# The mLSTM stage of a decoder layer: the next head's K and Q slabs inside a head, the recurrence in pieces between matmuls, states on ScalarE's DMA queue

## What is computed

```python
def _mlstm(q, k, v, i_pre, f_pre, C0, n0, m0):      # per head: q, k 128 wide, v 256 wide
    q = q * (DK ** -0.5)
    def step(carry, inp):                           # one chunk
        C, n, m = carry
        qx, kx, vx, ix, lfx = inp
        b = jnp.cumsum(lfx, axis=-1)
        dlog = jnp.where(causal, b[..., :, None] - b[..., None, :] + ix[..., None, :], -jnp.inf)
        inter = b + m[..., None]
        m_row = jnp.maximum(inter, jnp.max(dlog, axis=-1))
        dw = jnp.exp(dlog - m_row[..., None]); w_inter = jnp.exp(inter - m_row)
        s = jnp.einsum('bhld,bhjd->bhlj', qx, kx) * dw
        num = w_inter[..., None] * jnp.einsum('bhld,bhde->bhle', qx, C) + jnp.einsum('bhlj,bhje->bhle', s, vx)
        nq = w_inter * jnp.einsum('bhld,bhd->bhl', qx, n) + jnp.sum(s, axis=-1)
        h = num / jnp.maximum(jnp.abs(nq), jnp.exp(-m_row))[..., None]
        dec = jnp.exp(b[..., -1] + m - m_row[..., -1])
        wk = jnp.exp(ix + b[..., -1:] - b - m_row[..., -1:])
        C_new = dec[..., None, None] * C + jnp.einsum('bhl,bhld,bhle->bhde', wk, kx, vx)   # n likewise
        return (C_new, n_new, m_new), h
...
ha = _head_rms(ha).reshape(B, T, W_A_V) * g_norm_a * jax.nn.sigmoid(o_a)   # q, k, v, o_a: slices of rmsnorm(x) @ w_in
```

## Time and profile before

| | |
|---|---|
| time, median of 3 runs | 2891.81 us (2891.54 to 2893.38) |
| the profiled execution's own time | 2893.21 us |
| its span | 2891.5 us |
| PE busy | 2632.0 us (91%) |
| PEld busy | 2541.4 us (88%) |
| DVE, ACT, POOL busy | 1156.5, 639.4, 622.6 us (40%, 22%, 22%) |
| `mlstm`, first dense matmul to last output transpose | 978.81 to 1444.43 us of the span |
| mean granted TensorE clock | 0.957 of full |

### The profile page before, as it was taken

How to read it: one execution, slowest core, us unless ns; L and a number is a source line. 1 busy time by engine, 2 the same in 40 slices (tenths; PEclk the granted TensorE clock), 3 DMA queues, 4 the chain that set the end, 5 groups by cost and what they waited for, 6 DMA issues and landing times.

```text
span 2891.5 us, 40600 instructions
## 1 busy us (share of the span) xinstructions
PE 2632.0 (91%) x16191; PEld 2541.4 (88%) x16191; DVE 1156.5 (40%) x1932; ACT 639.4 (22%) x1319; POOL 622.6 (22%) x322
## 2 busy tenths in 40 slices
PE   4379999999999689899779999999999999999997
PEld 2269999999998689788679999999999999999997
DVE  2455655565554132523531141554323223134434
ACT  3235545554554111111100000001001000011112
POOL 2232121212120111111031131342212212112421
PEclk7679999999999899999889999999999999999998
DMA  3021221222110314223141121211111111111211
GB/s 122 17 78 55 63 61 32 71 66 61 32 53 24 84 30 92 49 72 85 20 121 46 44 99 44 105 44 44 44 44 44 49 40 49 47 38 45 74 30 70
DMA packets 235748, 165.23 MB, mean 57 GB/s; under 512 B 23643, under 2 KB 222875, under 8 KB 235583
## 3 DMA queue, kind: packets, MB, share of 16 engines
q1 hardware_dynamic: 235638, 163.64, 20.2%
HBM read 135.84 MB, written 27.76 MB: 57 GB/s over the span
## 4 chain that ended last, share of the span: by engine, by line
PE 45%; DVE 2%; issue 1%; POOL 1%; DMA 1%; ACT 0%; POOLq 0%; DVEq 0%; ACTq 0%
PE bank L227 40%; PE bank L239 4%; PE bank L2247 1%; DVE t_rlo L2383 0%; DMA t_w_raw<-in_w_in_dram 0%; PE bank L2284 0%; POOL t_w_lo L216 0%; DVE t_rhi L2380 0%; DVE hlo L2409 0%; DVE hhi L2406 0%; POOL t_rlo L2095 0%; DMA t_rraw<-HB 0%; PE bank L2159 0%; DVE hraw L2553 0%; DVE t_x L2475 0%
## 5 line engine op out<-in xcount | busy, mean ns | idle before, releaser
L216 POOL TENSOR_TENSOR t_w_lo<-t_w_raw,t_w_hi 128x1024 fp32r<-128x1024 f32 x112 | 270.1, 2412 | 942.6 <-DVE t_w_hi L211 942.6
L227 PE MATMUL bank<-t_rhi,t_w_lo 128*128 128x384 f32 (+1 forms) x1248 | 408.4, 327 | 2.8 <-issue 2.8
L227 PE MATMUL bank<-t_rhi,t_w_hi 128*128 128x384 f32 (+1 forms) x1248 | 408.0, 327 | 0.0
L227 PE MATMUL bank<-t_rlo,t_w_hi 128*128 128x384 f32 (+1 forms) x1248 | 407.9, 327 | 0.0
L227 PE MATMUL bank<-hhi,t_w_lo 128*128 128x384 f32 (+1 forms) x1224 | 400.1, 327 | 2.6 <-POOL t_w_lo L216 2.6
L227 PE MATMUL bank<-hhi,t_w_hi 128*128 128x384 f32 (+1 forms) x1224 | 400.3, 327 | 0.0
L227 PE MATMUL bank<-hlo,t_w_hi 128*128 128x384 f32 (+1 forms) x1224 | 400.1, 327 | 0.0
L227 PE MATMUL bank<-hhi,b_w_lo 128*128 128x384 f32 (+1 forms) x768 | 270.7, 352 | 10.1 <-POOL b_w_lo L216 10.1
L227 PE MATMUL bank<-hlo,b_w_hi 128*128 128x384 f32 (+1 forms) x768 | 252.6, 329 | 0.0
L227 PE MATMUL bank<-hhi,b_w_hi 128*128 128x384 f32 (+1 forms) x768 | 252.3, 329 | 0.0
L227 PEld LDWEIGHTS bank<-t_rhi,t_w_lo 128*128 128x128 f32 x1248 | 235.1, 188 | 3.5 <-issue 3.3
(11 more groups left out here) (371 smaller groups left out, 4333.0 us busy)
## 6 DMA issues: line engine op xcount, KB each, us to landing
b_w_raw<-in_w_in_dram SPq DMA_DIRECT2D x32, 512.0 KB, 4.0
t_w_raw<-in_w_up_dram SPq DMA_DIRECT2D x32, 512.0 KB, 3.8
t_w_raw<-in_w_down_dram SPq DMA_DIRECT2D x32, 512.0 KB, 3.8
a_w_raw<-in_w_in_dram SPq DMA_DIRECT2D x24, 512.0 KB, 3.9
t_w_raw<-in_w_in_dram SPq DMA_DIRECT2D x16, 512.0 KB, 3.6
b_gam<-ROWS_B SPq DMA_DIRECT2D x8, 576.0 KB, 4.9
b_eg<-ROWS_B SPq DMA_DIRECT2D x8, 576.0 KB, 3.8
b_kb<-ROWS_B SPq DMA_DIRECT2D x8, 576.0 KB, 3.6
```

The lines of the kernel that those rows point to most:

```text
L216: pool.tensor_tensor(self.lo[j % 2][:, 0:kt, :], self.raw[j % self.rs][:, 0:kt, :], self.hi[j % 2][:, 0:kt, :], ALU.subtract).then_inc(sel ...
L227: ins = pe.matmul(out, a[:, k, :], b[:, k, :], start=(start and k == 0 and i == 0), stop=(stop and k == kt - 1 and i == 2))
```

## The change

All of it is in `mlstm`. The slabs get names (`K_`, `Q_`, `VA_`, `VB_`, `OA_`, `OB_`), and:

- The turn of head h now makes VA, VB, OA, OB of head h and K, Q of head h+1. K and Q of head 0 stand ahead of the turns with a bank order of their own (`FB`), and the last head has one too (`LB`). TensorE waits for ScalarE's copies of Q ahead of the first and of the last turn.
- `scan_all` becomes a generator, `scan_steps`. `woven` makes a product group in pieces of 9, 9 and 6 matmuls and runs one step after each: 8 chunks and the sample chunk in OB's nine pieces, the 8 sample products in K's. In the last head the sample products stand bare.
- `matrices` for three chunks follows each group of OA; `outputs` of head h-1 follows each group of VA(h). The gated outputs are written into the gate's buffers instead of V0 and V1. VectorE's and GpSimd's work is ordered accordingly.
- ScalarE issues the loads of the sample states (`states`) and the four state stores (`store_states`), on its own DMA queue. SP keeps slabs, rows and output stores. The decay scalars of all heads are loaded once (`DALL`). In the last head the state stores come after the norms' exponential.

The core of the diff:

```diff
+            def order(nxt):
+                slots = dense(VA_) + dense(VB_)
+                for t in range(3):
+                    slots += [("dense", OA_, t)] + [(n, t) for n in ("kt", "va", "vb", "p")]
+                return slots + dense(OB_) + (dense(K_) + dense(Q_) if nxt else [])
...
-                HT = [V0, V1]
+                HT = OG
...
                         def turn(h, later, nxt):                      # SP
-                            if later:
-                                stores(h - 1)
...
+                            slab(h, OA_)
+                            if later:
+                                store_out(h - 1)
+                            slab(h, OB_)
+                            if nxt:
+                                wait(sp, dx, h, 3)
+                                row(h + 1, 0)
+                                slab(h + 1, K_)
+                                wait(sp, qi, h, 1)
+                                row(h + 1, 1)
+                                slab(h + 1, Q_)
+                                slab(h + 1, VA_)
+                                slab(h + 1, VB_)
...
+                        def woven(r, h, j, g, steps):                 # TensorE
+                            for _ in group(r, h, j, g, (3, 6)):
+                                next(steps, None)
+                            next(steps, None)
...
+                        def turn(h, later, nxt):                      # TensorE
                             for g in range(NG):
+                                whole(h, h, VA_, g)
+                                if later:
+                                    outputs(h - 1, g)
+                            for g in range(NG):
+                                whole(h, h, VB_, g)
+                            for g in range(NG):
+                                whole(h, h, OA_, g)
+                                if g == 0:
+                                    for n in range(NG):
+                                        taken(pe, h, ("dense", VB_, n))
+                                matrices(h, g)
+                            steps = scan_steps(h)
+                            for g in range(NG):
+                                woven(h, h, OB_, g, steps)
+                            if nxt:
                                 for g in range(NG):
+                                    woven(h, h + 1, K_, g, steps)
                                 for g in range(NG):
+                                    whole(h, h + 1, Q_, g)
+                            else:
+                                for _ in steps:
+                                    pass
...
+                        def turn(h, later, nxt):                      # ScalarE
+                            weights(h)
+                            for g in range(NG):
+                                copy_out(h, VA_, g)
+                            for g in range(NG):
+                                copy_out(h, VB_, g)
+                            if later:
+                                wait(act, s_st, h - 1, 4)
+                                states(h)
+                                wait(act, s_ha, h - 1, 2)
+                            for g in range(NG):
+                                copy_out(h, OA_, g)
+                            for c in range(2):
+                                numerator(h, c)
+                            copy_out(h, OB_, 0)
...
+                            numerator(h, NC)
+                            if nxt:
+                                for g in range(NG):
+                                    copy_out(h, K_, g)
+                                for g in range(2):
+                                    copy_out(h, Q_, g)
+                            row_norms(h)
+                            if nxt:
+                                copy_out(h, Q_, 2)
+                            store_states(h)
+                        states(0)
...
                         def turn(h, later, nxt):                      # VectorE
+                            split(h, VB_, h - 1, Q_)
+                            if later:
+                                wait(dve, og, h - 1, 1)
+                            exponents(h)
+                            if later:
+                                for t in range(3):
+                                    out_gate(h - 1, t)
+                            split(h, OA_, h, VA_)
+                            split(h, OB_, h, VB_)
+                            for t in range(3):
+                                matrices(h, t)
+                            queries(h)
+                            if nxt:
+                                split(h + 1, K_, h, OA_)
+                            for c in range(NC):
+                                state(h, c, later)
+                            sample_values(h)
+                            if nxt:
+                                split(h + 1, Q_, h, OB_)
+                            sample_states(h)
+                            if nxt:
+                                split(h + 1, VA_, h, K_)
+                            row_sums(h)
+                            gates(h)
+                            scaled(h)
```

More of the change, by code:

```diff
@@ L1714, in _, with claim, filled, group @@
                     def _(pe):
-                        def group(h, j, g):
+                        def claim(h, slot, *needs):
+                            banks, turn = ring(h)
+                            return banks.claim(pe, turn, slot, *needs)
+                        def filled(ins, h, slot):
+                            ring(h)[0].filled(ins, slot)
+                        def group(r, h, j, g, cuts=()):
                             a, w = GROUPS[g]
```

321 lines of the change are left out of this document (180 added, 141 removed).

## The result

The changed kernel takes 2863.39 us (median of 4 runs, 2861.85 to 2867.06) against 2892.47 for the kernel before on the same chip (2891.54 to 2893.38): a ratio of 0.9901, 95% interval 0.9885 to 0.9917. The gain is 29 us. The forecast was 2842 with a range of 2830 to 2862, so the sign was right, the size was 21 us too large, and the result lies just above the range.

The account below looks back on a forecast made before the run. TensorE was taken to bound the stage (465.6 us): 83.4 lost less 25.0 staying gives 58.4; less 2.5 (start) and 6.3 (end), 49.6. So 2893.21 becomes 2843.6, median 2842; range 2830 to 2862, 0.85 or so.

Parts of the forecast that it names:

- 382.2 us of work and 83.4 us lost: Of the stage's 465.6 us on TensorE, 382.2 were counted as work and 83.4 as lost; 25.0 of those would stay.
- The count of VectorE's and ScalarE's time from the start of VA: Within a head, both engines would deliver in time; tightest at the second output group's bank, 104 us, 1 us late costing 3.
- Rivals 2, 5 and 6: Returns at 0.19 us each, 2854 (0.11); recurrence still waits, 2867 (0.05); ScalarE stuck at stores, 2895 or more (0.03).
- the returns: TensorE going from small fp32 products back to dense matmuls: 80 times 0.04 us, 3.2 in all, 15.2 at the other end.
- The slow clock at the start: After the pause at the stage's start TensorE runs at its lower clock level; 2.3 us stay lost.
- the last head's end: After the last head's sample chunk no next slab lies beside the work; 17.0 us stay lost, 16.6 with the earlier gate.
- The gate put earlier: In the last head the first gated output needn't wait for ScalarE's exponential: -0.4 us.
- Two waits for Q's copies: New TensorE waits for ScalarE's copy of Q before the first and last turn: 0.7 us each, 1.4.
- The start: First K slab lands later as ScalarE loads the first sample states beside it: +2.5 us, between 0 and 5.9.
- The end: Last head's `n_sample` store, issued later, lands 6.3 us after the outputs did before: +6.3 us, between +4 and +9.
- The third rival, a slab comes late: OA's slab meets the previous head's stores on two queues; covered if landing at 11 us, otherwise about +12, 2854; chance 0.12.
- The working's other case: If the larger store shares turns too, OA's slab lands after 18 to 22 us, 2 to 6 late, three times, about +12.

## Why the prediction was wrong, by its own steps

**The work and what goes.** 382.2 us of work and 83.4 us lost were the frame, and it holds. Where no slab is late a head takes 95.8 to 96.7 us, and 96 to 98 was forecast. The waits before the output transposes, for `a_kw` and for the second state are gone. The count of VectorE's and ScalarE's time from the start of VA, with its tightest place at 104 us, was good enough: no wait for `a_o`, for a bank of the outputs or for a state appears. Rivals 2, 5 and 6 did not occur. The first dense step after small products is 0.26 us instead of 0.17, as the timeline of head 0 shows behind a group of `matrices`. But the returns don't cost 0.09 each over a whole head: six slabs and the small products are 95.5 us by the prediction's unit times, and a head with no late slab takes 95.8 to 96.0 (96.7 with the wait for Q's copy), so 23 returns cost 0.5 us or less, where 0.9 was taken.

```profile
1036.01 0.42 PE L227 MATMUL bank<-hhi,a_w_lo 128*128 128x384 f32 x1
1036.27 0.33 PE L227 MATMUL bank<-hlo,a_w_hi 128*128 128x384 f32 x1
1036.44 0.33 PE L227 MATMUL bank<-hhi,a_w_hi 128*128 128x384 f32 x1
```

**The slow clock at the start and the last head's end.** The last head's end takes 22.80 us, from its first sample product to the last transpose, where it took 22.49 and 22.1 was taken. The transposes wait 10.8 us as before. The gate put earlier did what was said: the wait of 0.44 for the first gated output is gone. But the last twelve sample instructions take 4.68 us instead of 3.57, with the granted clock at the lower level from 1380.0 for 3.4 us.

**Two waits for Q's copies.** 0.73 and 0.72 us, 1.5 together, against 1.4.

**The start.** +2.5 was taken; the pause went from 12.04 to 13.85, +1.8. That it comes from the sample states' loads is shown by the kernels that load them later: 11.93 and 12.02.

**The end.** +6.3 was taken, +6.5 measured. The number is partly luck. The store was issued at 1391.1 and landed 20.9 us later, as worked out, but the outputs were to have landed before it; they took 15.0 us beside it and landed last, 1.8 us behind it.

**The third rival, a slab comes late.** This is the first step that failed, by its chance and by one term of its working. The working priced the small store at 7.3 us, the difference between the landing of the 1 MB and that of the store behind it, and so had the slab land 11 us after its issue, "covered". A difference of two landings on one queue isn't the second one's own time. Before, the pieces of `n_sample` begin 11.2 to 12.3 us ahead of its landing, when most of the 1 MB isn't yet marked as done. And ahead of the 1 MB stands another small store that the working didn't price, the 128 pieces of `n` with 7.5 to 8.4 us from issue to landing. Measured in the changed kernel, the slab lands 19.5 to 20.7 us after its issue: 5.5 to 6.7 us until its first packet, the rest beside the 1024 pieces. The working's other case, in which the 1 MB shares, gave 18 to 22 us and 2 to 6 us late, three times, +12; measured are 1.8 to 4.3 us late, three times, and with the slow clock +14. That is a near hit by luck, since the kernel without the 1 MB has the same waits. The forecast held 0 for this term, and the rival had 0.12.

**What no step held.** The other 10 us lie outside the stage: the change moves the start of `tail`'s loop within its block of instructions, from 69 to 206, and each of the loop's two back jumps then pauses 2.8 to 2.9 us longer, for one more block of instructions, and pays for a slow clock behind it. This is the second step that failed: the path behind the stage was put at nothing, without a reason. Nothing in the prediction looked past the next stage's first DMA, though the order of the built program and a row with "issue" as releaser at each back jump were there to be read.

The sum, from the forecast: 49.6 of gain, less 14.0 for OA's slabs, less 10.0 in the tail, makes 25.6; the measured 29.7 in the profiled executions is 4.1 better. Of that, some 2.5 lie in the stage (a gain of 46.9 + 14.0 = 60.9 against 58.4), 0.5 in the start and the end, and 1.1 ahead of the stage, where nothing changed.

## What to carry to other kernels

Before a store in pieces of a few bytes is moved to a second queue, list what the first queue will have in flight during its whole landing time, and price the meeting by pieces, not by bytes. Count every such store in the row, the short ones too. Such a store belongs in a stretch in which no load is due, and at a stage's end it belongs first, ahead of everything that doesn't need it. And when an edit changes how many instructions an engine has ahead of a loop, look where the loop's start comes to lie in its block of instructions, since back jumps far from the edit can pay for it.

## What the runs showed of the hardware

- A back jump of TensorE pauses 0.9 to 1.6 us with the loop's start at offset 0 or 69 of a block of 256 instructions and 3.7 to 4.5 at 206. There two blocks of instructions are fetched before its next matmul instead of one. Of these jumps only the last kind lets the granted clock fall to its lower level, which nearly doubles the price: some 11 us for two jumps.
- A store of 1024 pieces of 4 bytes, issued 0.5 to 1.1 us behind one of 128 such pieces, lands some 21 us after its issue with or without 1 MB between them. While they last a load of 0.5 MB on another queue lands in 14 to 21 us instead of 4, and the stage's outputs in 11 to 15 instead of 3 to 5. Leaving out the 1 MB had no effect that could be measured.
- An instruction that only waits, and needn't, costs TensorE 0.10 to 0.11 us (137, 119 and 50 of them in three kernels, estimates from the times of the last matmul, the outputs' landing and the next DMA, or of the memset and the first matmul). Behind a stage's last matmul the stores can hide it.
